# Scan of a hybrid attention and RWKV-7 layer: new instruction orders for even and odd half-steps on TensorE, VectorE and ScalarE, one counter per member instead of one for both

## What is computed

```python
def step(S, inp):
    r_t, w_t, k_t, v_t, a_t, b_t = inp
    sa = jnp.einsum('zdhij,zdhj->zdhi', S, a_t)
    S = S * w_t[..., None, :] + sa[..., :, None] * b_t[..., None, :] + v_t[..., :, None] * k_t[..., None, :]
    y = jnp.einsum('zdhij,zdhj->zdhi', S, r_t)
    return S, y
...
_, y = lax.scan(step, S0, xs)
```

## Time and profile before

| | us |
|---|---|
| median of 3 runs | 2611.35 |
| lowest and highest | 2605.24 to 2615.7 |
| the profiled execution | 2609.12 |
| its span, from the first to the last instruction | 2607.2 |
| the scan within it | about 877 to 1500 |

### The profile page before, as it was taken

The page is one execution under the profiler, slowest core; times in us unless marked ns, Lnnn a source line. Parts: engine busy times, 40 slices in busy tenths (PEclk is TensorE's granted clock), DMA queues, the critical chain, the costliest instruction groups (busy, mean ns, idle before and its releaser), DMA issues. The chain is left out here.

```text
span 2607.2 us, 62791 instructions
## 1 busy us (share of the span) xinstructions
PE 2386.8 (92%) x27732; PEld 1950.8 (75%) x27732; DVE 1194.1 (46%) x2426; ACT 678.6 (26%) x1572; POOL 807.5 (31%) x623
## 2 busy tenths in 40 slices
PE   7999999999999677777787789999999999999997
PEld 6785568888888466666666667878888888888885
DVE  4105660000333566665666575564444444444446
ACT  5115661111111344545444332210111001110013
POOL 3322112222231233333333265022433223323234
PEclk9999999999999799999999989999999999999998
DMA  6110011112110100000000062211111011111014
GB/s 165 45 33 18 1 50 72 66 73 73 34 40 25 51 12 12 12 12 16 12 12 12 8 236 89 96 57 42 40 41 41 33 33 49 41 41 33 33 65 145
DMA packets 42282, 128.33 MB, mean 49 GB/s; under 512 B 12064, under 2 KB 12064, under 8 KB 40864
## 3 DMA queue, kind: packets, MB, share of 16 engines
q1 hardware_dynamic: 42016, 124.35, 14.4%
HBM read 96.24 MB, written 20.97 MB: 45 GB/s over the span
## 5 line engine op out<-in xcount | busy, mean ns | idle before, releaser
L2168 DVE TENSOR_TENSOR ff_f<-ff_f,ff_ps 128x512 f32<-128x512 f32 x300 | 205.3, 686 | 173.8 <-PE ff_ps L99 173.8
L2187 DVE TENSOR_TENSOR ff_sq<-ff_rl 128x512 f32<-128x512 f32 (+1 forms) x96 | 123.2, 1283 | 273.3 <-ACT ff_rl L2085 273.1
L2085 ACT ACTIVATE ff_rl<-ff_ps 128x512 f32<-128x512 f32 (+1 forms) x96 | 50.5, 526 | 754.8 <-PE ff_ps L99 754.8
L511 PE MATMUL sc_ps<-sc_xy,sc_ai 64*64 64x64 f32 x3200 | 123.6, 233 | 66.7 <-DVE sc_xy L1005 58.7
L1954 POOL TENSOR_TENSOR ff_wd0h<-ff_wdr,params 128x1024 fp32r<-128x1024 f32 x16 | 30.3, 1893 | 460.0 <-DMA ff_wdr<-in_w_down 460.0
L511 PEld LDWEIGHTS sc_ps<-sc_xy,sc_ai 64*64 64x64 f32 x3200 | 89.4, 138 | 82.4 <-DVE sc_xy L1005 64.1
L1105 DVE TENSOR_TENSOR sc_q<-sc_ps,sc_cs 128x128 f32<-128x128 f32 x400 | 98.1, 275 | 98.9 <-PE sc_ps L511 98.1
L862 ACT ACTIVATE sc_xy<-sc_ps 128x256 f32<-128x256 f32 x320 | 109.2, 381 | 126.4 <-PE sc_ps L527 116.5
L99 PE MATMUL ff_ps<-hh,ff_wu0h 128*128 128x512 f32 (+1 forms) x384 | 136.6, 356 | 4.8 <-issue 4.8
L99 PE MATMUL ff_ps<-hl,ff_wu0h 128*128 128x512 f32 (+1 forms) x384 | 136.5, 355 | 0.0
L99 PE MATMUL ff_ps<-hh,ff_wu0l 128*128 128x512 f32 (+1 forms) x384 | 136.4, 355 | 0.0
(11 more groups left out here) (321 smaller groups left out, 6732.6 us busy)
## 6 DMA issues: line engine op xcount, KB each, us to landing
ff_wur<-in_w_up SPq DMA_DIRECT2D x32, 512.0 KB, 3.5
ff_wdr<-in_w_down SPq DMA_DIRECT2D x32, 512.0 KB, 4.3
gwr<-in_w_in SPq DMA_DIRECT2D x31, 512.0 KB, 3.5
gm_dram<-gp_gm SPq DMA_DIRECT2D x8, 1280.0 KB, 4.4
ff_m<-gm_dram SPq DMA_DIRECT2D x16, 640.0 KB, 7.5
sc_sw<-sc_ar SPq DMA_DIRECT2D x40, 129.0 KB, 2.3
fr_x<-in_x SPq DMA_DIRECT2D x10, 512.0 KB, 4.8
ff_xs<-in_x SPq DMA_DIRECT2D x10, 512.0 KB, 4.5
```

Source lines behind the costliest of these rows:

```text
L511: last = nc.tensor.matmul(q_at(l, g, u)[on(rows, side), :], AI[g][on(rows, u), u, :], x_in(l, g, u)[on(rows, u), :], start=True, stop=True)
L2085: nc.scalar.activation(rl[v % 2][:, 0:tn], ps[:, b, 0:tn], ACT.Relu).then_inc(relu, 1)
L2168: nc.vector.tensor_tensor(own, own, ps[:, 4 + v % 4, :], ALU.add).then_inc(added, 1)
L2187: nc.vector.tensor_tensor(sq[v % 2][:, 0:tn], rl[v % 2][:, 0:tn], rl[v % 2][:, 0:tn], ALU.mult).then_inc(squared, 1)
```

## The change

The loop body with conditions is replaced on PE, DVE and ACT by two functions, `even(t)` and `odd(t)`. Every instruction of before is still issued, once and with the same shape; POOL and SP are as they were. `q_ps`, `q_ready`, `xy_ps` and `xy_ready` become a pair of semaphores each, one per member. `begin` is split into `unit` (L995 before) and `first_y` (L999 before), which can stand apart. `state` stays on DVE.

```diff
-        x1_ready, q_ps, q_ready, xy_ps, xy_ready, s_sum = (
-            sem("x1"), sem("q_ps"), sem("q"), sem("xy_ps"), sem("xy"), sem("s_sum"))
+        x1_ready, s_sum = sem("x1"), sem("s_sum")
+        q_ps, q_ready, xy_ps, xy_ready = (
+            [sem(f"{n}{m}") for m in range(HALF)] for n in ("q_ps", "q", "xy_ps", "xy"))
...
             def token_copy(q, g):
                 n = q * GR + g
-                act.wait_ge(tok_ps, n + 1)
                 act.wait_ge(masked, n + 1)
+                if n >= GR:
+                    act.wait_ge(y_ps, n - GR + 1)
...
+            def even(t):
...
+                products_q(t, 0, 0)
+                solve(t, 0)
+                gram_taken(done)
+                if t > 1:
+                    norms_taken(t - 1)
+                if pieces:
+                    piece_out(ct, i, 0, TOK_BANK)
+                products_q(t, 0, 1)
+                solve_u(t, 0)
+                products_xy(t, 0, 0)
+                products_xy(t, 0, 1)
+                solve_s(t, 0)
+                products_q(t, 1, 0)
+                if pieces:
+                    taken(ct, i, 1)
+                gram(t, 0)
+                products_q(t, 1, 1)
+                solve_o(t, 0)
+                products_xy(t, 1, 0)
+                products_xy(t, 1, 1)
+                solve(t, 1)
...
+            def odd(t):
...
+                if ahead:
+                    gram_taken(done)
+                    lora_products(q + 2)
+                products_q(t, 0, 0)
+                products_q(t, 0, 1)
+                solve(t, 0)
...
+                products_xy(t, 4, 0)
+                norm_sums(t)
+                products_xy(t, 4, 1)
```

The orders of VectorE, `even` whole and the end of `odd`:

```diff
+            def even(t):
...
+                joined(t, 0, 0)
+                joined(t, 0, 1)
+                side(t, 0, TOK_BANK)
+                if late:
+                    cumulate(q + 1, 0)
+                    cumulate(q + 1, 1)
+                joined(t, 1, 0)
+                joined(t, 1, 1)
+                stated(t, 0)
+                norm_part(t, 0)
+                collected(t, 0)
+                gram_masked(t, 0)
+                joined(t, 2, 0)
+                gram_unit(t, 0)
+                joined(t, 2, 1)
+                norm_part(t, 1)
+                side(t, 2, GRAM_BANK)
+                joined(t, 3, 0)
+                side(t, 1, TOK_BANK)
+                joined(t, 3, 1)
+                stated(t, 1)
+                norm_part(t, 2)
+                gram_first(t, 0)
+                gram_turn(t, 0)
+                gram_masked(t, 1)
+                joined(t, 4, 0)
+                joined(t, 4, 1)
+                norm_part(t, 3)
+                gram_unit(t, 1)
+                gram_first(t, 1)
+                gram_turn(t, 1)
+                collected(t, 1)
```

More of the change, by code:

```diff
@@ L949, in high_half @@
+                copy(t, 3, 1)
+                gram_tokens(t, 1)
+                copy(t, 4, 0)
+                copy(t, 4, 1)
+                if i == 0 and ct + 1 < CT:
+                    k_norm(ct + 1, TOK_BANK)
+                if i == 1 and ct > 0:
+                    y_std(ct - 1, GRAM_BANK)
+            for t in range(0, PAIRS, 2):
+                even(t)
+                odd(t + 1)
+            even(PAIRS)
             def high_half(ct):
```

444 lines of the change are left out of this document (238 added, 206 removed).

## The result

The changed kernel takes **2637.3 us** (median of three runs, 2635.73 to 2642.94) against 2611.35: a ratio of 1.011, 95% interval 1.009 to 1.013. It is 26 us slower. The forecast was 2591, in a range to 2628: wrong in sign and outside the range, on the side of the rival that gave 2635.

The account below looks back on a forecast made before the run. The prediction took a chain from engine to engine as the bound, no engine being full. Its terms, -39 + 7 + 5 + 7 = -20 us, gave 2591 us, with an 8-in-10 range of 2558 to 2628.

Parts of the forecast that it names:

- the rival that gave 2635: Even half-steps: PE stops for `outputs` ahead of level 1, held product delays both members' levels, about 2.2 each; chance 0.17.
- steps (a) to (c) of the odd half-steps: Odd half-steps: earlier beginning gains 0.5, lora products covering PE's transpose wait 1.05, u_copy behind fewer tanh 0.8 us.
- Odd half-steps, -1.95 each: The 20 odd half-steps: each falls from 14.7 to 12.75 us, -39 us together.
- Even half-steps with pieces, +0.45 each: The 15 even half-steps with pieces: a loss of 0.45 us each, +7 us together.
- Step (b): Even half-steps with pieces: piece 0's DVE part and cumulates precede level 1's joins, `outputs` its products; loss 0.6 us.
- The price of a hit: DVE product of two SBUF tensors under a POOL operation: costs 0 to 1.05 us more, taken as 0.85.
- step (c): Even half-steps with pieces: one `unit` under POOL, and both decays ahead of member 1's level 2 copy; loss 0.7 us.
- Even without pieces, +1.0: The 5 even half-steps without pieces: no piece to cover (a)'s gain, level 1's joins await cumulates; +1.0 each, +5 us.
- Sums, +1.2 each: Six norm sums moved to the odd half-step's end: table load and root delay the next p_copy; +1.2 each, +7 us.
- Semaphores and waits at nothing: New semaphores and dropped or added waits: cost nothing, bounds 0 to 0.1 us a half-step.
- The rival that the even half-steps give back what the odd ones gain: Even half-steps lose 1.0 us more each, so the sum is zero: 2600 to 2622 us; chance 0.20.
- The rival that fewer hits come: DVE products miss POOL's operations, or half of the hits occur: gain of 40 to 60 us, 2560; chance 0.20.

Follow-up runs that it names:

- e2: Changed kernel with the new order kept in odd half-steps only, even ones in the order of before: 2594.0 us, ratio 0.9935 to the kernel before.
- e4: Changed kernel with `outputs` waiting only for the state's addition, not the product behind it, no order changed: 2616.0 us, ratio 1.0028 to before.
- e15: Changed kernel with POOL's products by neg and two long bonus operations released by a pair's second transpose, not its first: ratio 1.0095 to before.
- e16: Changed kernel with the edits of e4, e9 and e15 together: ratio 1.0009 to before.
- e17: Changed kernel with the second member's last level 4 product issued four times in odd half-steps: 2648.2 us, ratio 1.0133 to before.
- e9: Changed kernel with piece 0 and the wait for the norms' root moved behind level 0's products in even half-steps: 2628.5 us, ratio 1.0087 to before.
- e1: Changed kernel with the norm sums back in the middle of the odd half-step, root ahead of the copy of level 3: 2644.8 us, ratio 1.0127 to before.
- e0: Changed kernel with the old order on PE, DVE and ACT, keeping the new semaphores and waits: 2608.6 us against 2608.1 for the kernel before.
- e13: Changed kernel with POOL's two products by neg on a quarter of the columns, part of the computation left out: ratio 1.0058 to before.
- e8: Changed kernel with both cumulates moved behind the first state's operations in even half-steps: 2653.8 us, ratio 1.0183 to before.
- e10: e2 and e4 together, against the kernel before: 2586.2 us, ratio 0.9929.

## Why the prediction was wrong

**What bounds the kernel** was read rightly: a chain from engine to engine, and PE's waits for the transposes and for `u_copy` as its clearest losses. Both went, as the steps (a) to (c) of the odd half-steps said (48.4 to 3.3 and 20.0 to 1.1 us).

**Odd half-steps, -1.95 each:** -1.54 for the plain ones in the mean, -1.37 between those at full clock in each kernel (14.72 and 13.35). Right in kind, a quarter too large by the mean: some 8 us of the error. e2, the odd order alone, is 14 us faster than before.

**Even half-steps with pieces, +0.45 each:** this is the step that failed. The nine that don't follow sums took 2.68 more. With their five neighbours behind sums they are 55 of the 66 us that even half-steps lost, where the sum had 7, and 7 more for the sums. Three things stand in its place.
- Step (b) had the products of level 1 start 1.2 later behind `outputs`, and took half of it back, to 0.6, since the held product had made level 2 late before as well. After, that product is hardly held, and PE stops all the same: 21 times by 1 us in 480 us, with the products of a level behind it, whose joins DVE and whose copies ACT wait for. e4 shows what can be won at that wait alone: 21 us of the kernel, and 0.6 per half-step in two with pieces that are at full clock in every kernel (t = 20 and 30: 15.1 and 15.2 before, 16.3 and 16.2 after, 15.8 and 15.6 in e4).
- The hold fell on another operation. The forecast had the state's product at a mean above 0.6, and `unit` above 0.45; they came at 0.40 and 0.62. The price of a hit was right (0.85; the 31 long ones of `unit` lost 0.8 each), and one such hit was in step (c) as a part of 0.7. But it lies at the end of the even half-step, ahead of the second transpose, and the bonus operations (2.89 each), which no step of the sum names, fall there too. Without it t = 20 and 30 take 15.4 and 15.6 (e15): some 0.8 of their 1.1. That and e4's 0.6 are more than the whole together, so they overlap. And it buys the odd half-steps' early gram: e15 shows the trade to be even.
- TensorE's clock was left out. The three even half-steps with pieces at full clock take 16.40, the six others 19.56, with 7.4 us at 1.2 GHz each. These 3.2 x 6 = 19 us are the largest part by size (before, three of the nine had a fall and took 0.8 more, so some 17 us of it are new), but only a correlation. It doesn't follow PE's idle time: before has 131 us of that in the 39 half-steps with 49 at 1.2 GHz, the change 106 with 80, and e16 106 with 22. e17 did not move it. Whether a stop at some place brings the clock down, or something else does both, stays open.

The three edits of e16 take these nine to 15.55, below before; which part of that is the clock's no run separates. The 31 us of the five behind sums are less well known: e16 still has 19.21 there.

**Even without pieces, +1.0:** of the five that it names, the four that don't follow sums (t = 4, 6, 10 and 38) took 1.0 more each. Right. The fifth, t = 2, is behind sums and took 7.2 more.

**Sums, +1.2 each:** by the table's means a pair of an odd half-step with sums and the even one behind it takes 33.80, a plain pair 32.05, so 1.75 more; before 31.38 and 30.91, 0.47 more. The net is +1.3, so the size was right, except at t = 2. So was its way: the last join of t = 23 ends at 1254.06 and `p_copy` comes at 1257.52, 3.5 behind it, and behind the six sums it is 2.7 to 3.6, where 3.6 was forecast (1.1 behind t = 19, without sums). What the forecast had not: the piece waits 2.3 for the root too, with the second member's first product behind it. e9 shows no gain from removing that, and e1 that the old place costs as much.

**Semaphores and waits at nothing:** right, e0.

**The rivals.** The slower one named the place and the price: 2.2 more for each even half-step, 2.65 in all with pieces, where the nine took 2.68, and 2635 for 2637. The last is partly luck, since it had 3.2 more for each even half-step without pieces, of which four took only 1.0. Its cause fell: the product is hardly held (6.7 us in all, 20.1 before), and the wait stays when POOL's two products are cut to a third of their time (e13). By the rows it is late because the joins of both members, the cumulates and the addition stand ahead of it in DVE's queue (that the cumulates alone do it, e8 does not bear out), at t = 20 in the changed kernel:

```profile
1195.87 1.26 DVE L1054 TENSOR_TENSOR_SCAN sc_cum<-sc_cs,sc_lw 128x256 f32<-128x256 f32 x2
1197.05 0.26 DVE L1181 TENSOR_TENSOR sc_q<-sc_ps,sc_cs 128x128 f32<-128x128 f32 x1
1197.48 0.29 DVE L1181 TENSOR_TENSOR sc_q<-sc_ps,sc_cs 128x128 f32<-128x128 f32 x1 [0.16 <-PE sc_ps L512]
1197.68 0.28 DVE L1091 TENSOR_TENSOR sc_s<-sc_ps,sc_s 128x128 f32<-128x128 f32 x1
1198.00 0.29 DVE L1093 TENSOR_TENSOR sc_s<-sc_s,sc_sw 128x128 f32<-128x128 f32 x1
```

```profile
1198.35 0.34 PE L601 MATMUL sc_ps<-sc_gm,sc_tk 64*64 64x64 f32 x8 [0.93 <-DVE sc_s L1093]
```

The rival that the even half-steps give back what the odd ones gain put the point of balance at 1.0 more each; they gave back more. The rival that fewer hits come, for a gain of 40 to 60, fell: the state's product, `unit` and `first_y` were held for 39 us together, where they were for 25.

## What to carry to other kernels

Read a new order from the queue of the engine that everyone waits for: for each instruction moved ahead there, ask when its input is ready and what stands behind it, and then try the stop away, since its length does not give its price: 20 us less of waiting for the state made the kernel 21 us faster in one order (e4), and 10 us less nothing in another (e10). Where one event releases another engine's work, see which of the first engine's instructions it will fall upon, in both kinds of half-step, and what comes late if it is released later: here the two prices were equal. When an order helps one kind of stage and harms another, try each alone: the odd half alone was 0.7% faster than before, the whole 1.1% slower.

## What the runs showed of the hardware

- TensorE's clock fell behind short stops, but not behind each: one of 1.90 us was followed by over 6 us at 1.2 GHz, in which a piece of 1.12 us took 2.07; behind one of 2.32 us the product ran at full clock. Of 39 half-steps 30 ran wholly at 2.4 GHz before and 24 after; of the changed kernel's nine even ones with pieces, not behind sums, those with a fall were 3 us longer.
- A VectorE addition of two SBUF tensors was held for 1.95 us (2.23 in place of 0.28) by one GpSimd operation of 2.89 us, and ended 0.14 behind it; a mask and a join under the same operation, which read PSUM, were not held.
- The table load ahead of the root took 1.28 us, and the root began 0.02 behind its end.
- Less waiting and less time are not the same: in e4 PE waited 20.0 us less for the state and the kernel was 21 us faster; in e10 10.1 us less than in e2, and the ratio stayed within the intervals. Against before, the changed kernel's PE idled 25 us less in the 39 half-steps and was 23 us slower there.
